# First stage's projections as three f32r products a weight chunk, and attention's keys chosen by a bitwise search for the threshold

## The reference

```python
# first block, layer 0: RWKV-7 time mixing on h = rms_norm(x), 1024 tokens, width 1024, inner width 2048
xx = token_shift(h) - h
xr, xw, xk, xv, xa, xg = (h + xx * mu[j] for j in range(6))
r, k, v, g = xr @ w_in[0], xk @ w_in[1], xv @ w_in[2], xg @ w_in[3]
y = wkv7_scan(r, decay, k, v, kk, kk * a)          # a recurrence per head of 64
x = x + (group_norm(y) + bonus) * silu(g) @ w_out  # then layer 1: gated short convolution, final norm

# second block: q, latent c, index q/k/w, gates from one product; S5 branch beside attention
index_score = sum_h w_idx[t, h] * relu(q_idx[t, h] . k_idx[s])     # 8 index heads of 32
_, sel = top_k(where(s <= t, index_score, -max), 256)              # per query t
att = softmax over the 256 chosen causal keys, 8 heads, keys and values the latent c
ssm = GLU(gelu(s5(u)))
out = layer_norm(alpha * x + concat(att * silu(ga), ssm * silu(gs)) @ w_out)
```

## Time and profile before

| | |
|---|---|
| median of 3 runs | 4590.96 us (4587.19 to 4592.53) |
| the profiled execution | 4586.48 us, span 4584.8 us |
| PE busy | 4219.0 us, 92% of the span |
| DVE busy | 2370.4 us, 52% |
| ACT, POOL busy | 1315.9 us and 274.1 us |
| TensorE's mean granted clock | 0.938 of full speed |

### The profile page before, as it was taken

The page is one execution under the profiler, slowest core; times in us unless marked ns, Lnnn a source line. Parts: engine busy times, 40 slices in busy tenths (PEclk is TensorE's granted clock), DMA queues, the critical chain, the costliest instruction groups (busy, mean ns, idle before and its releaser), DMA issues. The chain is left out here.

```text
span 4584.8 us, 131580 instructions
## 1 busy us (share of the span) xinstructions
PE 4219.0 (92%) x58346; PEld 3217.2 (70%) x58346; DVE 2370.4 (52%) x5302; ACT 1315.9 (29%) x3044; POOL 274.1 (6%) x308
## 2 busy tenths in 40 slices
PE   7999999999999999998988999999969977877579
PEld 5888888888888888886777887888746643444344
DVE  4556555565555655554215543444255533688842
ACT  2233323332323223222213332232113312433221
POOL 1000000000000000000000000000000000111100
PEclk9999999999999999998999999999989988566789
DMA  2322222222222222221413333333211110000010
GB/s 74 92 68 79 63 88 68 83 64 78 77 79 68 79 68 77 70 79 50 127 37 110 96 96 83 101 96 96 55 42 28 23 37 9 1 1 0 0 46 37
DMA packets 520412, 289.54 MB, mean 63 GB/s; under 512 B 30256, under 2 KB 509728, under 8 KB 519904
## 3 DMA queue, kind: packets, MB, share of 16 engines
q1 hardware_dynamic: 519904, 281.88, 21.3%
HBM read 267.55 MB, written 12.58 MB: 61 GB/s over the span
## 5 line engine op out<-in xcount | busy, mean ns | idle before, releaser
L344 PE MATMUL a_bank<-a_lerps,a_wt 128*128 128x256 f32 x4096 | 1036.9, 393 | 2.4 <-DVE a_lerps L815 2.4
L344 PEld LDWEIGHTS a_bank<-a_lerps,a_wt 128*128 128x128 f32 x4096 | 731.0, 189 | 126.9 <-issue 21.2
L1208 PE MATMUL b_bank<-b_hR,b_wR 128*128 128x512 f32 x1024 | 399.8, 390 | 15.5 <-DVE b_wL L1213 15.5
L1208 PE MATMUL b_bank<-b_hL,b_wR 128*128 128x512 f32 x1024 | 399.7, 390 | 0.0
L1208 PE MATMUL b_bank<-b_hR,b_wL 128*128 128x512 f32 x1024 | 399.5, 390 | 0.0
L931 DVE TENSOR_TENSOR a_iv_X<-a_bank,a_iv_X 128x256 f32<-128x256 f32 x256 | 108.7, 425 | 413.3 <-PE a_bank L448 413.3
L1213 DVE TENSOR_TENSOR b_wL<-b_w,b_wR 128x1024 fp32r<-128x1024 f32 (+1 forms) x144 | 192.4, 1340 | 116.8 <-ACT b_wR L1296 104.0
L692 ACT ACTIVATE a_iv<-a_bank 128x512 f32<-128x512 f32 x192 | 114.7, 597 | 419.1 <-PE a_bank L454 266.2
L1208 PEld LDWEIGHTS b_bank<-b_hR,b_wR 128*128 128x128 f32 x1024 | 193.0, 188 | 56.0 <-issue 16.1
L1208 PEld LDWEIGHTS b_bank<-b_hL,b_wR 128*128 128x128 f32 x1024 | 192.9, 188 | 40.4
L1208 PEld LDWEIGHTS b_bank<-b_hR,b_wL 128*128 128x128 f32 x1024 | 193.0, 189 | 40.2
(11 more groups left out here) (441 smaller groups left out, 8156.7 us busy)
## 6 DMA issues: line engine op xcount, KB each, us to landing
a_wt<-in_a_w_in SPq DMA_DIRECT2D x256, 512.0 KB, 4.2
b_w<-in_b_w_in SPq DMA_DIRECT2D x128, 512.0 KB, 4.0
b_w<-in_b_w_out SPq DMA_DIRECT2D x16, 1024.0 KB, 5.6
rwkv_out<-a_ybuf SPq DMA_DIRECT2D x64, 128.0 KB, 5.7
m_w<-in_a_w_out SPq DMA_DIRECT2D x16, 512.0 KB, 4.0
s_wp<-in_w_in SPq DMA_DIRECT2D x12, 512.0 KB, 3.8
a_xtok<-in_x SPq DMA_DIRECT2D x4, 1024.0 KB, 7.1
m_two<-rwkv_out SPq DMA_DIRECT2D x16, 256.0 KB, 3.0
```

The source lines that it names most:

```text
L344: r = mm(o, wt[:, j, c, :], src[:, c, :], start=(c == 0), stop=(c == ND - 1))
L1208: m = nc.tensor.matmul(o, a, b, start=(first and i == 0), stop=(last and i == 2))
```

## The change

In the first stage the four projections become R/L products: three f32r matmuls a chunk in place of one f32 matmul. ACT rounds the weights of the next piece (`round_weights`), DVE subtracts (`low_weights`), in places written into the step. The lerps are made in steps 14 and 15 of the pass before, as 16 units of two pieces each: DVE multiplies into one of three tiles `tmp`, ACT rounds it (`round_lerp`), POOL subtracts (`low_lerp`); there is one buffer for them, not two. SP loads a projection's weights when its subtraction is done. The save of the state on DVE moves behind the first two masks of the next step.

In the second block the index scores of query blocks 2 to 7 are formed in the GELU iterations, ten pieces each: PE a matmul, ACT a relu, DVE a multiply-add. The keys are chosen by a search: the threshold's 32 bits are set from the top, each by counting the scores at or above it. Blocks are searched in pairs (2,3), (4,5), (6,7). Bits are placed: 8 before the GLU's evictions, 15, 13 and 6 after its first three, 6 in attention's preparation, 16 in slots 0 to 15, 32 in slots 12 to 43. `choose` then builds the mask in slots 4 to 6, with a running count to settle ties. Index matmuls, their relu, scale and POOL sums leave the slots.

```diff
@@ rwkv_block, PE
-                        r = mm(o, wt[:, j, c, :], src[:, c, :], start=(c == 0), stop=(c == ND - 1))
+                        mm(o, wR[name][:, c, :], lerpR[name][:, c, :], start=(c == 0), stop=False)
+                        mm(o, wR[name][:, c, :], lerpL[name][:, c, :], start=False, stop=False)
+                        r = mm(o, wL[name][:, c, :], lerpR[name][:, c, :], start=False, stop=(c == ND - 1))
@@ rwkv_block, ACT
+                def round_weights(m, names=LERPS):
+                    for name in names:
+                        act.wait_ge(s["w" + name], 16 * (m + 1))
...
+                        a(wR[name][:, :, :], wt[name][:, :, :], ACT.Copy).then_inc(s["wR"], 1)
+                def round_lerp(ps, name, i):
...
+                    a(lerpR[name][:, 2 * i:2 * i + 2, :], tmp[n % 3][:, :, :], ACT.Copy).then_inc(s["hi"], 1)
...
                     copy_two(trs[:, 0:2, :, :], 7, "trAB_out")
                     if m is not None:
                         rates(m, e)
+                    lerps(15, ("r", 2), ("r", 3), ("g", 0))
                     act.wait_ge(s["pE2"], ready)
                     copy_two(iv2, 2, "S2E2")
...
                         decays(m, e)
+                    lerps(15, ("g", 1), ("g", 2), ("g", 3))
                     act.wait_ge(s["pE8"], ready)
                     copy(iv["E2"], 2, "E8")
                     if m is not None:
                         keys(m, e)
+                            round_weights(m + 1, "k")
...
+                    lerps(14, ("k", 0), ("k", 1), ("k", 2))
+                    lerps(15, ("v", 0), ("v", 1), ("v", 2), ("v", 3))
                     act.wait_ge(s["pP12"], ready)
                     copy_two(pr12, 4, "P12", scale=-1.0)
+                    lerps(14, ("k", 3), ("r", 0), ("r", 1))
@@ rwkv_block, POOL
+                def low_lerp(ps, name, i):
...
+                    low(lerpL[name][:, pair_of, :], tmp[n % 3][:, :, :], lerpR[name][:, pair_of, :]).then_inc(s["lo"], 1)
@@ rwkv_block, DVE
+                def low_weights(m, names):
+                    for name in names:
+                        v.wait_ge(s["wR"], m * len(LERPS) + LERPS.index(name) + 1)
+                        tt(wL[name][:, :, :], wt[name][:, :, :], wR[name][:, :, :].bitcast(F32), ALU.subtract).then_inc(s["wL"], 1)
...
                     if m is not None:
                         columns(m, e2, m % NF)
+                        low_weights(m, "gv")
+                    if prep and at == 15:
+                        lerped(prep, ("g", 1), ("g", 2), ("g", 3))
                     add_to_x("X2", "pX2", "X1")
...
                         bonus_keys(m, e2)
+                    if prep and at == 14:
+                        lerped(prep, ("k", 0), ("k", 1), ("k", 2))
+                    if prep and at == 15:
+                        lerped(prep, ("v", 0), ("v", 1), ("v", 2))
...
                         gate(m, e2)
+                            low_weights(m + 1, "kr")
+                    if prep and at == 14:
+                        lerped(prep, ("k", 3), ("r", 0), ("r", 1))
...
+                    if prep and at == 14:
+                        lerped(prep, ("r", 2), ("r", 3), ("g", 0))
@@ s5_block, g_: the search, the pieces
+class Search:
+    def bit(self, v, g, i):
+        for b in GROUPS[g]:
...
+            nc.vector.tensor_scalar(self.junk[self.counted % 2][:, 0:keys(b)], score_of(sel, b), sel["thr"][:, col].bitcast(F32), None,
+                                    ALU.is_ge, ALU.add, accum_out=sel["cnt"][:, col]).then_inc(s["count"], 1)
...
+        nc.vector.tensor_scalar(sel["flip"][:, cols], sel["cnt"][:, cols], TOPK - 0.5, -1.0 if i == 0 else 2.0 ** place, ALU.is_lt, ALU.mult).then_inc(s["flip"], 1)
+        v.wait_ge(s["flip"], self.updated)
+        nc.vector.scalar_tensor_tensor(sel["thr"][:, cols], sel["flip"][:, cols], (1 << 30) if i == 0 else (1 << place) >> 1, sel["thr"][:, cols],
+                                       ALU.bitwise_xor, ALU.bitwise_xor).then_inc(s["thr"], 1)
+            pieces = [(b, h, t) for b in range(B0, NB) for h in range(IH) for t in halves(b)]
+                    def logits(n):
+                        b, h, t = pieces[n]
+                        if n >= 2:
+                            pe.wait_ge(s["rl"], n - 1)
...
+                        nc.tensor.matmul(bank[n % 2][:, HALF:HALF + t.stop - t.start], qiT[rows, h // 4, b * P:(b + 1) * P], kiT[rows, t], start=True, stop=True).then_inc(s["logit"], 1)
...
                     for j in range(SUB):
+                        for n in range(j * PER, (j + 1) * PER):
+                            logits(n)
                         pe.wait_ge(s["gelu"], j + 1)
@@ attention_block, DVE
                     def choose(b, h):
-                        for i in range((h - 1) * steps // parts, h * steps // parts):
-                            ch(nc.vector.max(top[:, :], sc))
-                            ch(nc.vector.match_replace(sc, top[:, :], sc, LEAST))
...
+                        if h == AH - 4:
...
+                            ch(ts(up, sc, t, None, ALU.is_gt, ALU.add, accum_out=above[:, i:i + 1]))
+                            ts(room[:, i:i + 1], above[:, i:i + 1], -UNIT, TOPK * UNIT, ALU.mult, ALU.add)
+                            ch(ts(eq, sc, t, UNIT, ALU.is_equal, ALU.mult))
+                        if h == AH - 3:
+                            ch(nc.vector.tensor_tensor_scan(up, eq, eq, 0.0, ALU.add, ALU.bypass))
+                            ch(stt(eq, up, room[:, i:i + 1], eq, ALU.is_le, ALU.mult))
+                        if h == AH - 2:
+                            ch(ts(out, sc, t, -UNIT, ALU.is_le, ALU.mult))
+                            ch(tt(out, out, eq, ALU.add))
...
+                        if k < len(BITS_1):
+                            search.bit(v, 1, BITS_1[k])
+                        if 0 <= k - SLOT_2 < 32:
+                            search.bit(v, 2, k - SLOT_2)
```

More of the change, by code:

```diff
@@ L1845, in s5_block, with halves, last_piece @@
             sg = sb("sg", [P, SEQ])
+            kiT = sb("kiT", [P, SEQ])
+            wi = sb("wi", [P, NB, IH])
+            rl = sb("rl", [P, 4, HALF])
+            qiT = latent[:, 1:3, :]
+            def halves(b):
+                parts = 1 if keys(b) <= HALF else 2
+                return [slice(i * keys(b) // parts, (i + 1) * keys(b) // parts) for i in range(parts)]
+            pieces = [(b, h, t) for b in range(B0, NB) for h in range(IH) for t in halves(b)]
+            PER = len(pieces) // SUB
+            def last_piece(b):
+                return max(n for n, piece in enumerate(pieces) if piece[0] == b)
             with nc.Block() as block:
@@ L1896, in _, with relu @@
                 def _(act):
+                    def relu(n):
+                        b, h, t = pieces[n]
+                        wide = t.stop - t.start
+                        act.wait_ge(s["logit"], n + 1)
+                        if n >= 4:
+                            act.wait_ge(s["acc"], n - 3)
+                        nc.scalar.activation(rl[:, n % 4, 0:wide], bank[n % 2][:, HALF:HALF + wide], ACT.Relu).then_inc(s["rl"], 1)
+                    nc.scalar.activation(qiT, qiT, ACT.Copy, scale=IDIM ** -0.5).then_inc(s["qi"], 1)
                     for j in range(SUB):
@@ L2052, in _ @@
                     stt(cT[:, :], latent[:, 0, :], kvg[:, 0:1], rs[:, :], ALU.mult, ALU.mult).then_inc(s["cT"], 1)
+                    for i in BITS_PRELIM:
+                        search.bit(v, 1, i)
                     for k in range(NQ):
@@ L2065, in sb3 @@
                 return sub.enter_context(nc.sbuf_tensor("tb_" + name, shape, dt))
-            rl = [sb3(f"rl{i}", [P, SEQ]) for i in range(2)]
-            score = [sb3(f"score{i}", [P, SEQ]) for i in range(2)]
-            top = sb3("top", [P, 8])
+            same, upto = sb3("same", [P, SEQ]), sb3("upto", [P, SEQ])
+            above, room = sb3("above", [P, NI]), sb3("room", [P, NI])
             mb = [sb3(f"mb{i}", [P, SEQ]) for i in range(2)]
@@ L2095, in scores @@
                         m.then_inc(s["sc"], 1)
-                    def index(k):
-                        b, h = divmod(k, IH)
-                        pe.wait_ge(s["pT"], k + 1)
-                        rows = slice((h % 4) * IDIM, (h % 4 + 1) * IDIM)
-                        for t in pieces(keys(b + B0)):
-                            m = nc.tensor.matmul(tp[:, t], qiT[rows, h // 4, (b + B0) * P:(b + B0 + 1) * P], kiT[rows, t], start=True, stop=True)
-                        m.then_inc(s["logit"], 1)
                     def turn(k):
```

359 lines of the change are left out of this document (222 added, 137 removed).

## The result

The changed kernel takes 4455.5 us (median of 4 runs, 4451.7 to 4460.1), the kernel before in the same comparison 4589.1 (4586.5 to 4592.5): ratio 0.9709, 95% interval 0.9692 to 0.9726, or 133.5 us less. The forecast was 4328 with a range of 4225 to 4430. So it is faster, but by half of what was forecast, and outside the range.

A forecast was written before the change was run, and what follows sets the result against it. It took TensorE to bound the first stage and choosing keys on DVE to bound attention; -112 + 80 + 8 + 14 - 253 = -263 from 4586.5 gave 4323.5, about 4328 as median; own range 4270 to 4385, 80% range 4225 to 4430.

The forecast's parts named there:

- I count 0 for 60 steps: First stage: added DVE subtractions (4.6 us) and ACT copies (4.2 us) a step hide in DVE's waits, costing 0.
- The six steps at the ends of passes: First stage, steps 14 and 15: making the next pass's lerps costs 3 x 11 = 33 us, bounds 0 and 60.
- The late S2E2, E8 and v: Step 15, first stage: S2E2 3.7 us late, E8 2.6 more, v units on POOL 3.3 more; 9.6 together.
- The record price: First-stage projections: an f32r record of 256 columns takes 0.120 us, bounds 0.112 to 0.227.
- part 1: First-stage projections as three f32r matmuls a chunk: -145 us, +33 at pass ends, so -112 for the stage.
- rivals D: First-stage projections: load and stream do not overlap, a record keeps 0.227 us, +500 us, 4973; chance 0.04.
- E: First-stage projections: the record is at the load floor of 0.112 us, 48 less, 4280; chance 0.30 shared with rival A.
- rival B: First stage: added DVE and ACT work becomes the limit, steps stay at 32.3 us, 145 us lost, 4473; chance 0.09.
- Part 2: Index scores moved beside the GELU: score loop ends at 3828 against 3748, +80 us, bounds +50 and +130.
- rival C: Score loop beside the GELU: the clock stays half throughout, +50 us, 4378; chance 0.11.
- Part 3: Key choice by bitwise search: +8 us in the GLU, +14 before attention's loop, -253 in it (299 against 552).
- rival A: Key search: counting runs at two elements a cycle, 4289 in total; chance 0.30 shared with E.

The follow-up runs named there:

- Experiment 4: Changed kernel with its first-stage weight loads moved out of the stretch 3 to 10 us into a step, all bytes kept: 4353.8 us.
- experiment 7: Changed kernel with ACT and DVE making the r units before the decay chain in the first pass: 4453.5 us.
- experiment 2: Changed kernel with every first-stage weight load after the first step cut to one of eight row blocks, at the same places: 4359.3 us.
- e1_bunch: Kernel before with its r, g and v weight loads issued together after the v projection: 4595.1 us against 4587.8.
- e3_bunch_dense: Kernel before with its r, g and v weight loads issued together at the start of a step, after the low-rank matmuls: 4692.0 us against 4588.7.

## Why the prediction was wrong, step by step

**The step that failed** is the cost of nothing for the edits of an ordinary step: "I count 0 for 60 steps". For the four weight loads I asked only whether they land in time ("over half a step before use; a landing takes some 4 us"), and they do. I did not ask what they run into. SP's list has r behind the low-rank rows, which wait for PE's low-rank matmuls; so r, g and v go out together at the start of the step, onto the small matmuls of the inverse. The first stage by its own parts, from the two traces (us against before):

- 55 ordinary steps: forecast 55 x -2.30 = -126.5, measured -16.3. Here are 110 of the 155 us. Of the 2.0 that are missing a step, 1.5 went as idle time marked issue and 0.5 as longer busy time of PE, where its clock fell after a gap. Experiment 4 gives 1.7 a step back by moving loads alone.
- The six steps at the ends of passes: forecast 33 - 6 x 2.3 = +19, measured +36.8; a pair takes 41.2 + 43.7 us. The late S2E2, E8 and v were found where I walked (PE waited 2.8, 2.3, then 2.4 and 1.9 us). A pair took 5.9 us more than forecast, as a mean of the three, and most of it is a term that I set too low, the clock's answer to the waits: I allowed 1.4 us. PE is idle for 11.2 us a pair, 1.6 more than the 9.6 that I walked through, but it is busy for 72.7 us where the forecast was 67.0 (71.6 before, less twice 2.3); its granted clock was 0.84 in the second step of each. That is 4.3 us over what I allowed. Not seen either: DVE and POOL slow each other; what that costs of the time no run shows. The subtraction of 1024 columns, 1.22 us elsewhere, beside POOL's work:

```profile
566.62 1.99 DVE L900 TENSOR_TENSOR a_wL_k<-a_wt_k,a_wR_k 128x1024 fp32r<-128x1024 f32 x1
568.53 2.28 DVE L900 TENSOR_TENSOR a_wL_r<-a_wt_r,a_wR_r 128x1024 fp32r<-128x1024 f32 x1
```

  and POOL's unit takes 1.46 where I had 1.30. The Trainium skill (GPSIMD Engine Reference, Key points) says that POOL shares its interfaces to the buffer with DVE, with contention where DVE reads two inputs from it; the trace agrees.
- The start: forecast 0, measured +27.4. I bounded it by POOL's own work, back to back. POOL stood still 9.9 us before r's units and 1.0 to 1.4 before every further group; PE's clock reads 0.67 from 50 to 90 us, with its gaps. Seven of the 27 came back in experiment 7, and four in experiment 4, where only the loads had moved.
- The last two steps: -4.6, measured -4.8.

**What held.** The record price, the number on which part 1 stood: start to start 0.120 us, as taken.

```profile
1207.34 0.28 PE L365 MATMUL a_bank<-a_lerpR_r,a_wL_r 128*128 128x256 f32 x1
1207.46 0.28 PE L363 MATMUL a_bank<-a_lerpR_r,a_wR_r 128*128 128x256 f32 x1
1207.58 0.28 PE L364 MATMUL a_bank<-a_lerpL_r,a_wR_r 128*128 128x256 f32 x1
```

So rivals D (0.227) and E (0.112) are out, and by experiment 2 rival B (DVE and ACT as the limit) is too, although its 32.3 us a step came true for another reason. The prediction had named the test, "I am wrong [...] if PE waits in ordinary steps"; it does, for what was on no list of mine.

Part 2: the GELU with the scores and the GLU together took 245.4 us against 159.6, +86 for +88. The score loop runs at clock 0.70 (row one), between the two levels as chosen, not at half (rival C), and ends at 3875, which is 3828 and the 45 us by which it started later:

```profile
3742.00:3867.00 125.00, 119.19 (x244) 50.10 (x245) 67.48 (x115) 47.99 (x92) 1.47 (x5) 0.70 0.11 38
3867.00:3988.00 121.00, 101.11 (x214) 42.88 (x212) 98.35 (x281) 12.17 (x15) 0.29 (x1) 0.90 0.00 0
```

Part 3: a counting pass costs what the max-reduce suggested, so rival A is out. Its row for attention (shortest, median and longest ns, then the forms):

```profile
L1625 DVE TENSOR_SCALAR_CACHE_REDUCE t_junk<-sel_score,sel_thr x96: 871/1146/1279, 4030.9 to 4221.6; 128x896 f32<-128x896 f32 x32, 128x1024 f32<-128x1024 f32 x32, 128x640 f32<-128x640 f32 x16, 128x768 f32<-128x768 f32 x16
```

1279 ns for 1024 columns, 871 for 640, so 1.06 ns an element, and 83 for reading the sum, against 1285 + 83 assumed. The Trainium skill (VectorE: DVE Perf Modes, The perf-mode tier table) gives fp32 tensor_scalar in SBUF a 2x mode, without a word on a summed output; with one the trace does not have it. The first five blocks of the loop took 22.6, 40.9, 35.9, 36.8 and 38.6 us where 27, 43, 37, 39 and 41 were forecast, and 5% more for waits, which were not needed: 175 for 196. The last three took 30.2, 33.3 and, to the end of the loop, some 44 for 33, 34 and 36. So 283 for 299. This part alone makes the change a gain.

## What to carry to other kernels

When a change moves or bunches DMA issues, ask not only whether each load lands in time but what runs beside it: where TensorE goes through many short matmuls, its instructions have to be fetched just as fast, and here a fetch beside a burst of loads began 2 us late. Idle time of TensorE marked issue, in the middle of a run that waits for nothing, and at multiples of one number of matmuls, was the sign of it in this kernel; the cure was to put the loads beside its long matmuls. And a speed-up of the long matmuls is not the place where such time shows: compare the stage's busy time with its length before asking which engine is the limit.

## What the hardware showed that I had not expected

- A block of 16,384 bytes of instructions let PE go on a median of 2.4 us after its fetch began, beside a burst of 330 to 350 GB/s as beside hardly a load; the burst delayed the beginning of the fetch, by a median of 2.0 us. One burst of three loads of 512 KB, moved by some 6 us (r's load goes out at 29.4 us of a step in e1_bunch, at 2.9 us of the next in e3_bunch_dense), made 97 us of difference (4595 and 4692 us).
- The f32r record of 256 columns repeats every 0.120 us at the full clock of 2.4 GHz, and every 0.213 at 1.2 GHz, as from 1273.0 us on in the third step shown, after the gap of 1.81 us.
- POOL's subtractions stretched DVE's from 1.22 to 1.99 and 2.28 us.
